# Inverse roots of five token norms: a sum and a power on GpSimd in place of a logarithm and an exponential on ScalarE

## What is computed

```python
h = layer_norm(ALPHA * h + mix, ln1_g, ln1_b)      # norm 1
h = layer_norm(ALPHA * h + moe(h), ln2_g, ln2_b)   # norm 2
u = rmsnorm(h, norm_mix_w)                         # norm 3
h = h + mixer_2(u)
v = rmsnorm(h, norm_ffn_w)                         # norm 4
h = h + conv_gated_mlp(v)
out = rmsnorm(h, final_norm_w)                     # norm 5

def rmsnorm(x, w):
    return x * rsqrt(mean(x * x, axis=-1) + 1e-5) * w
```

## Time and profile before

| | |
|---|---|
| median of three runs | 1875.41 us (1872.4 to 1879.01) |
| profiled execution, its own time | 1878.23 us |
| span of its profile | 1876.4 us, 26867 instructions |
| TensorE busy | 1757.6 us (94%) |
| VectorE busy | 703.1 us (37%) |
| ScalarE busy | 570.7 us (30%) |
| GpSimd busy | 65.6 us (3%) |
| mean granted TensorE clock | 0.966 |

### The profile page before, as it was taken

The page is one execution under the profiler, slowest core; times in us unless marked ns, Lnnn a source line. Parts: engine busy times, 40 slices in busy tenths (PEclk is TensorE's granted clock), DMA queues, the critical chain, the costliest instruction groups (busy, mean ns, idle before and its releaser), DMA issues. The chain is left out here.

```text
span 1876.4 us, 26867 instructions
## 1 busy us (share of the span) xinstructions
PE 1757.6 (94%) x11209; PEld 1214.6 (65%) x11209; DVE 703.1 (37%) x1191; ACT 570.7 (30%) x774; POOL 65.6 (3%) x50
## 2 busy tenths in 40 slices
PE   6989969999999999999999999949999998979997
PEld 6989854434444344344343443449999888979997
DVE  3668641211111122112111111153695554557643
ACT  4733510101111111011111110144564676356432
POOL 2003000000000000000000000000100111000000
PEclk9999968999999999999999999979999999989999
DMA  8344466999999999999999999924554432635542
GB/s 256 123 133 135 153 248 255 431 429 430 430 429 431 430 430 430 429 431 430 430 430 430 431 430 430 388 71 143 173 180 155 135 113 93 200 106 187 182 155 77
DMA packets 159862, 534.97 MB, mean 285 GB/s; under 512 B 5507, under 2 KB 123395, under 8 KB 127040
## 3 DMA queue, kind: packets, MB, share of 16 engines
q1 hardware_dynamic: 158560, 531.06, 71.9%
q0 software_dynamic: 1248, 3.14, 0.6%
HBM read 533.13 MB, written 1.05 MB: 285 GB/s over the span
## 5 line engine op out<-in xcount | busy, mean ns | idle before, releaser
L1098 PE MATMUL bank<-expert_weights,x_gathered 128*64 128x512 f32 x1536 | 338.5, 595 | 2.6 <-DMA expert_weights<-in_expert_w_up_dram 2.6
L106 DVE TENSOR_TENSOR m_w_lo<-raw_weights,m_w_hi 128x2048 fp32r<-128x2048 f32 (+1 forms) x120 | 278.6, 2325 | 162.5 <-ACT m_w_hi L102 161.3
L102 ACT ACTIVATE m_w_hi<-raw_weights 128x2048 fp32r<-128x2048 f32 (+1 forms) x120 | 227.2, 1894 | 134.6 <-PE bank L120 107.5
L1098 PEld LDWEIGHTS bank<-expert_weights,x_gathered 128*64 128x64 f32 x1536 | 106.7, 137 | 211.5 <-issue 200.9
L1114 PE MATMUL bank<-expert_weights_late,activations 128*64 128x512 f32 x1024 | 226.8, 595 | 0.0
L118 PE MATMUL bank<-u_hi,m_w_hi 128*128 128x256 f32 x704 | 202.6, 288 | 3.4 <-DVE u_lo L1429 3.4
L119 PE MATMUL bank<-u_lo,m_w_hi 128*128 128x256 f32 x704 | 200.7, 285 | 0.0
L120 PE MATMUL bank<-u_hi,m_w_lo 128*128 128x256 f32 x704 | 200.7, 285 | 0.0
L1005 DVE COPY step_cols<-expert_slots 128x2 f32 (+1 forms) x33 | 5.6, 169 | 445.3 <-PE bank L1081 445.3
L1032 DVE TENSOR_TENSOR pre_act<-bank,bias_now 128x512 f32<-128x512 f32 x64 | 44.0, 688 | 315.3 <-PE bank L1105 315.3
L1114 PEld LDWEIGHTS bank<-expert_weights_late,activations 128*64 128x64 f32 x1024 | 70.7, 137 | 130.1 <-issue 127.9
(11 more groups left out here) (376 smaller groups left out, 2669.8 us busy)
## 6 DMA issues: line engine op xcount, KB each, us to landing
expert_weights<-in_expert_w_up_dram SPq DMA_DIRECT2D x96, 2048.0 KB, 19.3
expert_weights_late<-in_expert_w_down_dram SPq DMA_DIRECT2D x64, 2048.0 KB, 17.6
raw_weights<-in_expert_w_up_dram SPq DMA_DIRECT2D x32, 2048.0 KB, 19.4
raw_weights<-in_w_in_dram SPq DMA_DIRECT2D x62, 1024.0 KB, 5.3
raw_weights<-in_w_up_dram SPq DMA_DIRECT2D x22, 1024.0 KB, 5.1
raw_weights<-in_w_s_out_dram SPq DMA_DIRECT2D x8, 1024.0 KB, 5.0
raw_weights<-in_w_down_dram SPq DMA_DIRECT2D x8, 1024.0 KB, 4.9
raw_weights<-in_w_out_dram SPq DMA_DIRECT2D x4, 1024.0 KB, 5.2
```

The costliest lines, as they stand in the source:

```text
L102: act.activation(self.s.w_hi[:, s, 0:size], self.s.raw[:, s, 0:size], ACT.Copy).then_inc(self.hi_done, 1)
L106: dve.tensor_tensor(self.s.w_lo[:, s, 0:size], self.s.raw[:, s, 0:size], self.s.w_hi[:, s, 0:size].bitcast(FP32), ALU.subtract).then_inc(s ...
L1098: m = pe.matmul(U[b][rows[half], :], lhsT=xg[:, 2 * u + a, :], rhs=w[:, a, 512 * c:512 * c + 512], start=(first and a == 0), stop=(last an ...
```

## The change

A helper for GpSimd computes the root in two instructions, the sum with epsilon and the power -0.5. It reads two constant columns, `s.eps_ln` and the new `s.minus_half`. All five norms use it, and the two ScalarE instructions of each tile go. In mixer 2 and in the FFN's first norm it stands behind GpSimd's DMA issues, in mixer 1 behind its last sum. `layer_norm` loses its parameter `per_tile`, since the semaphore now rises once per tile at both layer norms.

```diff
+def inverse_roots(pool, s, mv, at, eps_added, var_ready, n_ready, done):
+
+    pool.wait_ge(var_ready, n_ready)
+    pool.tensor_tensor(mv[:, at + 1:at + 2], mv[:, at:at + 1], s.eps_ln, ALU.add).then_inc(eps_added, 1)
+    pool.wait_ge(eps_added, n_ready)
+    pool.tensor_tensor(mv[:, at + 2:at + 3], mv[:, at + 1:at + 2], s.minus_half, ALU.pow).then_inc(done, 1)
...
 def layer_norm(...)
-        dve.wait_ge(rstd_ready, per_tile * (t + 1))
+        dve.wait_ge(rstd_ready, t + 1)
...
 # mixer 1, GpSimd
+                pool.memset(s.minus_half, -0.5).then_inc(half_set, 1)
...
+                pool.wait_ge(half_set, 1)
+                for t in range(TT):
+                    inverse_roots(pool, s, mv[:, t, :], 1, eps_added, var_ready, t + 1, ln_rstd)
...
 # mixer 1, ScalarE
-                for t in range(TT):
-                    act.wait_ge(var_ready, t + 1)
-                    own.add(act.activation(mv[:, t, 2:3], mv[:, t, 1:2], ACT.Ln, bias=s.eps_ln))
-                    own.wait()
-                    act.activation(mv[:, t, 3:4], mv[:, t, 2:3], ACT.Exp, scale=-0.5).then_inc(ln_rstd, 1)
...
 # experts, GpSimd (the same lines go from ScalarE)
+                for t in range(TT):
+                    inverse_roots(pool, s, mv[:, t, :], 1, eps_added, var_ready, t + 1, ln_rstd)
...
 # mixer 2, GpSimd, behind three dma_start (the same lines go from ScalarE)
+                for t in range(TT):
+                    inverse_roots(pool, s, mv[:, t, :], 2, eps_added, var_ready, t + 1, r_ready)
...
 # FFN, GpSimd, behind one dma_start (inverse_rms goes from ScalarE)
+                for j in range(2 * TT):
+                    inverse_roots(pool, s, mv[:, j, :], 2, eps_added, var_ready, j + 1, r_ready)
```

More of the change, by code:

```diff
@@ L143, in tokens_out, with layer_norm @@
     return m
-def layer_norm(dve, own, h, stats, mv, var_ready, rstd_ready, g, b, loaded, n_loaded, ready, per_tile=1):
+def inverse_roots(pool, s, mv, at, eps_added, var_ready, n_ready, done):
[3 more added lines that the diff above has]
+    pool.tensor_tensor(mv[:, at + 2:at + 3], mv[:, at + 1:at + 2], s.minus_half, ALU.pow).then_inc(done, 1)
+def layer_norm(dve, own, h, stats, mv, var_ready, rstd_ready, g, b, loaded, n_loaded, ready):
     for t in range(TT):
@@ L229, in mixer1 @@
         x_loaded, con_loaded, con1_loaded, small_loaded, ln_loaded = sem("x_loaded"), sem("con_loaded"), sem("con1_loaded"), sem("small_loaded"), sem("ln_loaded")
+        half_set, eps_added = sem("half_set"), sem("m1_eps_added")
         rows_zero, rows_loaded, cols_ready = sem("rows_zero"), sem("rows_loaded"), sem("cols_ready")
@@ L933, in experts @@
             "gather_mm", "gather_out", "scatter_mm", "scatter_out", "y_out", "scattered", "cleared", "bias_now_ready", "m2_dve_own"))
+        eps_added = sem("m2_eps_added")
         ln_loaded, gate_mm, gate_out, sum_ready, ln_own, var_ready, ln_rstd, h_ready = (sem(n) for n in (
@@ L993, in _ @@
                     act.activation(y_rows[:, :], U[0][:, :], ACT.Copy, scale=0.5).then_inc(y_out, 1)
[L994 to L998, removed]
             @block.vector
@@ L1197, in mixer2 @@
             "acum_mm", "shift_ready", "act_own", "dve_own", "pool_own"))
+        eps_added = sem("m3_eps_added")
         tap_done, xbc_ready, cv_ready, conv_a, ya_ready, ya_hi_done, ya_done = (sem("m3_" + n) for n in (
@@ L1290, in _ @@
                 own.add(act.activation(pick[:, :], C("identity")[0:N_HEADS, 0:N_HEADS], ACT.Copy))
[L1291 to L1295, removed]
                 for k in range(KD):
@@ L1729, in ffn @@
         (fw_loaded, var_ready, r_ready, diag_ready, vt_mm, vt_hi, vt_lo, tap_done, h1_ready, p_ready, p_hi_done, p_done,
-         act_own, dve_own, out_ready, stored) = (sem("m4_" + n) for n in (
+         eps_added, dve_own, out_ready, stored) = (sem("m4_" + n) for n in (
             "fw_loaded", "var_ready", "r_ready", "diag_ready", "vt_mm", "vt_hi", "vt_lo", "tap_done", "h1_ready", "p_ready",
-            "p_hi_done", "p_done", "act_own", "dve_own", "out_ready", "stored"))
+            "p_hi_done", "p_done", "eps_added", "dve_own", "out_ready", "stored"))
         DOWN = [(c, k) for c in range(4) for k in range(len(DOWN_K))]
@@ L1778, in _ @@
                 pool.dma_start(fw[:, :], A["final_norm_w_2"].partition_broadcast(P)).then_inc(fw_loaded, 16)
+                for j in range(2 * TT):
+                    inverse_roots(pool, s, mv[:, j, :], 2, eps_added, var_ready, j + 1, r_ready)
             @block.scalar
             def _(act):
[L1782 to L1788, removed]
                 split_hi(act, 0)
-                for t in range(TT):
-                    inverse_rms(t)
                 for k in range(KD):
@@ L1814, in _ @@
                     split_hi(act, n + 3)
-                for t in range(TT):
-                    inverse_rms(TT + t)
             @block.vector
@@ L1923, in whole_block @@
         s.eps = sb("eps", [P, 4])
-        s.eps_ln, s.eps_hg = s.eps[:, 0:1], s.eps[:, 1:2]
+        s.eps_ln, s.eps_hg, s.minus_half = s.eps[:, 0:1], s.eps[:, 1:2], s.eps[:, 2:3]
         s.gate = sb("expert_gates", [P, TT, N_EXPERTS])
```

2 lines of the change are left out of this document (1 added, 1 removed).

## The result

| | before | after |
|---|---|---|
| median of seven runs each, side by side | 1875.41 us (1872.4 to 1883.85) | 1865.33 us (1862.51 to 1871.97) |
| ratio after / before | | 0.9942 (95%: 0.9918 to 0.9966) |
| profiled execution, its own time | 1878.23 us | 1871.97 us |
| span of its profile | 1876.4 us | 1870.2 us |

The kernel is 0.58% faster, 10.9 us with an interval from 6.4 to 15.4 (0.0058, 0.0034 and 0.0082 of 1875.41). The forecast was 1866.9 us, "faster".

What follows compares the result with a forecast made beforehand. Waits for the inverse roots, not busy shares, were taken to matter, TensorE being busy 1757.6 of 1876.4 us. Terms 0.18 + 0.16 - 3.91 - 3.81 - 1.17 = -8.55 us from 1875.41 gave 1866.9, range 1862 to 1876.

Steps and rivals of the forecast that it cites:

- Path, not shares: Whole kernel: shares of busy time price nothing; what matters is whether anything waits for the inverse roots.
- The chain of 0.88 us: One tile's root on GpSimd: 0.08 + 0.19 + 0.08 + 0.50 + 0.03 us, from variance to reader.
- The slow power: Rival, all five places: a power of 2.40 us makes the kernel 7.1 us slower, 1882.5 us; chance 0.14.
- Norms 3 and 4: Mixer 2's norm and FFN's norm: second diagonal starts earlier, 3.91 and 3.81 us gained.
- Only the very first load of a place is hidden: ScalarE before the change: only a place's first table load, 1.28 us, is done ahead of the wait.
- Norm 5: Final norm: second tile's sum stands behind VectorE's two-input product, root out at 1870.89 against 1872.06, 1.17 us gained.
- The layer norms: Norms 1 and 2: 0.51 and 0.53 us gained, less 0.69 of VectorE held up; net 0.18 and 0.16 slower.
- The exclusion: GpSimd sums and VectorE instructions with two SBUF operands do not run together, whatever their size; seen for 1024 elements.
- No exclusion for tiny instructions: Rival, layer norms and final norm: tiny GpSimd instructions and VectorE don't exclude each other; -10.7 us, 1864.7; chance 0.10.
- The clock: Rival, mixer 2 and FFN: TensorE's low-clock stretches take 2.5 to 5 us back, 1869.4 to 1871.9; chance 0.09.
- one stretch less: TensorE's clock: one 5 us half-rate stretch fewer, worth 2.5 us, giving 1864.4 us.
- The first use: Rival, first layer norm: GpSimd's first power might wait for code, about 6 us, giving 1872.4; chance 0.04.

Runs made afterwards that it cites:

- RMS norms alone: Kernel before with only norms 3 to 5 moved to GpSimd, norms 1 and 2 left on ScalarE: 1869.62 us, ratio 0.9943.
- layer norms alone: Kernel before with only norms 1 and 2 moved to GpSimd, the others left on ScalarE: 1875.97 us, ratio 0.998.
- batched: Kernel before, all on ScalarE, with both tiles' logarithms ahead of both exponentials at each place: 1873.41 us, ratio 0.9973.
- experiment 4: Kernel after with each tile's power computed five times in a chain, only the last used: 1888.9 us, ratio 1.0053 against the kernel before.
- Experiment 5: Kernel after with unused GpSimd sums of 16, 64, 256 elements in mixer 1 and powers of 4, 32 in the experts: 1868.93 us, one time.

## Why the prediction was right

**Path, not shares: right.** TensorE is at 94% before and after, and the time fell by about what the waits lost. For the five kernels with an interval, the sum of the places against the timed change: after -10.3 against -10.9 (-15.4 to -6.4), RMS norms alone -9.0 against -10.7 (-14.8 to -6.6), layer norms alone -1.4 against -3.8 (-7.0 to -0.6), batched -2.7 against -5.1 (-7.7 to -2.3), five powers +10.8 against +10.0 (+6.6 to +13.2). All five lie inside, from a gain of 10 us to a loss of 11. The intervals are some 3 to 4.5 us to either side, so this tests the account to a few us and no better. In all five the timed change is 0.6 to 2.4 us lower than the sum. Where norm 4 is early, the clock behind it accounts for some 1.2 us of that; the other part can be the one set of runs before that four of the five share.

**The chain of 0.88 us: right.** Measured at norm 4 it is 0.93: 0.08 to the sum, 0.19, 0.08, 0.55 and 0.03 to the reader. The power, the one price that no row showed, is 0.55 for the chosen 0.50. Its bounds of 0.19 and 2.40 were wide, and the 0.50 was borrowed from another engine; that it came so near is in part luck. The slow power was not the case, but experiment 4 shows that it would have turned the sign.

**Norms 3 and 4: right,** 3.79 for 3.91 and 3.76 for 3.81. At norm 3 GpSimd's three DMA issues end at 1238.26, 1.02 us after the first mean square (1237.24), and not 0.60 after it as before; so the two roots follow one another without a gap, and the second is 1.00 after its mean square. GpSimd enters the stage 0.77 us behind VectorE (1236.22 and 1235.45), before it was 0.40. It is 0.77 in the kernel with the layer norms alone and 0.41 in that with the RMS norms alone, but 0.42 in experiments 4 and 5, whose GpSimd has most to do at the end of the experts; what sets it is open. With the RMS norms alone the chain was 0.99 all the same. One reading of the forecast is wrong, without effect on its sum: "Only the very first load of a place is hidden" holds at norms 1, 2 and 5, but at norms 3 and 4 ScalarE is still busy with L102 when the first mean square comes, and the first load starts behind it too (1236.73 against 1236.51, 1651.41 against 1651.29). That is why these two places took 4.79 and 4.69 us, and norm 5 only 3.30.

**Norm 5: right in mechanism, 1.40 for 1.17.** The second sum did stand behind L1867, as forecast: 1.16 us for 0.19. The forecast charged the whole 0.19 after L1867's end, but the sum ended 0.04 after it, and L1867 itself started 0.08 before the mean square's end and not 0.04 after it.

**The layer norms: the mis-sized term.** The step was "If the second tile's sum and power each get in ahead of one of them, they hold VectorE up for 0.19 + 0.50 = 0.69 us". It gave -0.18 and -0.16; measured were +0.68 and +0.70. Of the 0.86 us between them at norm 1, 0.69 are this term; the other 0.17 are that L164 started 0.13 earlier behind the statistics than forecast and took 0.77 instead of 0.81. The exclusion is there, but its cost falls on GpSimd: the sum and the power wait for VectorE, and their root is needed only at 256.96, while it is out at 256.20. The other direction was inferred from 1024 elements, where GpSimd's turn costs VectorE 2.2 us. Experiment 5 shows 0.30 us at 256 elements and nothing at 64, and the traces nothing at one. The Trainium skill's page "SBUF — State Buffer", section "SBUF: two separate sides", says that the pair goes to whoever starts first, for the whole instruction. The trace agrees where VectorE starts first, and it does not agree where GpSimd does: the power of 6.32 us did not delay the VectorE product that began 1.07 us into it. That row alone doesn't exclude that the power stood behind this product too; the powers of experiment 4, which end inside VectorE's next instruction, speak against it.

**The rivals.** "No exclusion for tiny instructions", forecast at 1864.7, came nearest in its time (1865.33), though the timing can't tell it from 1866.9. It had the layer norms right, where VectorE is held up by nothing, and norm 5 wrong, where the exclusion held. The clock took nothing back that the traces show as belonging to the change; behind norm 4 it went the other way and gave about 1.2 us, half of the 2.5 that the forecast set for one stretch less. The first use cost nothing: the very first power started 0.08 us after its sum's end, at 252.88, and took 0.57 us, the other undisturbed ones 0.55 to 0.56. The Trainium skill's page "GPSIMD Engine Reference", section "2.1 Instruction dispatch", gives about 6 us for a first call. They are not seen here; whether GpSimd's function was already in place by then, no run tells.

What was not tried: the sum with epsilon on VectorE, which would take 0.27 us out of each chain (0.19 and 0.08) and at most about 1.4 us in all, an estimate without the cost on VectorE, and below what a measurement of this kernel can tell.

## What to carry to other kernels

Look for small functions on the way between two large engines, and price there the table loads ahead of them, not the functions: here 1.28 us each for 0.2 to 0.3 us of work. A sum and a power on an idle GpSimd cost 0.9 us a tile with all waits, and this holds for one element per partition only, since each further element cost 0.16 to 0.19 us more. Check what the result's reader is: where a reader stands right behind the root (norms 3 and 4) the whole difference is gained, and where VectorE has other work (the layer norms) a few tenths.

## What the hardware showed that was not expected

- A GpSimd instruction waits for a VectorE instruction of 128x1024 that is under way, and it does so for a TENSOR_SCALAR with one tile as input (L164: the sum took 0.66 us instead of 0.19) as well as for products of two tiles (L166: the power 1.55 instead of 0.55) and for L1867 (the sum 1.16). It does not wait for the statistics: the first tile's sum and power took 0.19 and 0.57 beside them.
- The other way round, VectorE was not held up measurably by GpSimd instructions of 1, 16, 32 and 64 elements per partition, and for 0.30 us by one of 256. GpSimd's one-element powers end while VectorE's next instruction is under way (0.40 us after L167's end in experiment 4).
- The wait stands inside the instruction's busy time in the profile. GpSimd's busy time rose by 11.5 us, where ten sums and ten powers undisturbed are 10 x (0.18 + 0.55) = 7.3 us; 3.9 of the other 4.2 us are these waits (0.47 + 1.00 and 0.47 + 0.99 at the layer norms, 0.97 at the end).
- The same program's mixer 2 took from 392.70 to 399.97 us at a mean granted clock of 0.98 to 0.96, more than any one place gained. Only events inside one place could be compared to hundredths.
- The FFN's products began at a granted clock of 0.85 where TensorE had waited 10.3 us or more at norm 4, and of 0.92 to 1.00 where it had waited 6.5 to 7.7.
